# Two transformer blocks on one core: dummy matmuls and a split load ahead of the first unit, another order of steps around the two norms and in the second attention

## The chip, the cores and the metric

The kernel runs on one core of one Trainium2 chip. The metric is the device time of one execution in microseconds, from the chip's own clock; lower is better. TensorE does the matmuls and the transposes; VectorE (DVE), ScalarE (ACT) and GpSimd (POOL) do the work per element; SyncE (SP) and sometimes ACT and POOL issue the DMAs. Each engine works off its own list of instructions in the order written, and waits on semaphores where the program says so.

## The reference

Two blocks follow each other on an activation of 256 tokens x 2048 columns, all in fp32.

```python
def first_block(x, ...):
    h = rms_norm(x, pre_mix_g)
    a, gate, q, k, v = split(h @ w_in)
    yc = silu(layer_norm(depthwise_conv31(a * sigmoid(gate))))
    ya = neighbourhood_attention(q, k, v, rpb)          # 16 heads of 64
    x = x + rms_norm(concat(yc, ya) @ w_out, post_mix_g)
    h = rms_norm(x, pre_mlp_g)
    f = square(relu(h @ w_up)) @ w_down                 # 8192 wide
    return x + rms_norm(f, post_mlp_g)

def second_block(x, ...):
    h = rms_norm(x, norm_g)
    q_a, k_a, v_a, o_a, i_a, f_a, z_a, c_q, c_kv, k_r, z_b, g_a, g_b = split(h @ w_in)
    y_a = (sigmoid(o_a) * rms_norm(mlstm(...)) * silu(z_a)) @ w_a      # 8 heads
    q_b, k_b, v_b = latent_projections(c_q, c_kv, k_r)                 # norms, rotary part of 64
    y_b = (causal_attention(q_b, k_b, v_b) * silu(z_b)) @ w_b          # 16 heads
    return x + (sigmoid(g_a) * y_a + sigmoid(g_b) * y_b) @ w_out
```

## The kernel before

**Units.** All weights are cut into stripes of 512 output columns, and each stripe into units of 2 x 128 rows of the contraction: a tile of 128 x 1024 floats, 512 KB (one narrow stripe, "small", is cut otherwise). There are 734 units. Every one goes through the same four stations: SP loads it into one of 4 `raw` buffers; ACT writes its rounded high half `whi` (`split`); DVE writes the rest `wlo = raw - whi` (`low`); both have rings of 5. TensorE multiplies in `dense(u, j, tiles)`: for each of the two 128-row parts j and each of the two token tiles t, three matmuls of 128 x 512 (high x high, high x low, low x high). So a unit is 12 matmuls. The activations are held transposed in the same two halves, `ta_hi`/`ta_lo` and `tb_hi`/`tb_lo`.

**Order.** Nothing is scheduled at run time. Each engine's program walks through "slots", two for a unit; `E(name)` is the slot in which a stripe ends. All other work is written as generators ("sides") that yield the slot from which their next step may be issued; at each slot an engine first works off its sides, in the order of its list, and then the splits or lows of that slot. The order of the list decides who comes first within a slot, and an instruction that waits holds up all that is behind it on its engine.

**The beginning.** SP loads a piece of the transposed x (`xt`, 256 KB for two of its 16 rows of tiles) and unit 0, then the next piece and unit 1, and so on; ACT's queue loads `vec`, all small vectors in one table of 540 columns (270 KB). ACT then scales two tiles of xt by the gains in that table into `ta_hi` and splits unit 0; DVE makes `ta_lo` and `wlo`; then TensorE can start.

**The norms.** B1 is the first unit of the up projection, B2 that of the second block; b stands for either. The four units before b (TAIL) and the four from b on (HEAD) are multiplied tile by tile: first all four for token tile 0, then all four for tile 1. So the norm of tile 0 runs while TensorE works on tile 1, and the other way round. Steps of one norm for a tile t: DVE adds the last stripes' sums from PSUM (`finish`, L1566); ACT takes sums of squares; DVE and POOL form the root (`root`, L1443, L1444, L2105); DVE multiplies by the post gain (`gain`, L1560) and adds to x for each of four column chunks c (`add(t, c)`, L1597); TensorE transposes the chunk (L673); ACT writes `ta_hi` (L1068) and DVE `ta_lo` (`low_of(t, c)`, L1604). `NORM_TURNS` gives the slots, relative to 2b, of the eight (t, c): -2, -1, 2, 3, 5, 6, 8, 9. Two stripes end late before the first norm (mixq2, mixq3), one before the second (down73).

**The second attention.** For each of 16 heads TensorE forms scores (L797, L798), DVE masks and takes maxima (part "m", L1997 to L2002), ACT the exponentials (L1372), TensorE transposes them into PSUM bank 1 (L805), ACT copies, TensorE multiplies by v (L812 to L814), also into bank 1, and DVE scales the result out of it (part "x", L2016). Within DVE's list `uqr_side`, the rotary part of the queries of the second half (squares L1906 and L1908, then per tile t five operations L1930 to L1935), stands ahead of `at_side`.

## Time and profile before

| what | value |
|---|---|
| median of three executions | 2186.52 us (2183.7 to 2187.66) |
| the profiled execution: its time, its span | 2183.4 us, 2181.6 us |
| TensorE busy | 2157.3 us, 99% |
| DVE, ACT, POOL busy | 1345.7, 1078.5, 59.1 us |
| mean granted clock of TensorE | 1.000 |
| DMA | 419.9 MB, 192 GB/s over the span |

The span runs from the first to the last instruction in one profiled execution; the execution's own time is 1.8 us longer. Busy time of TensorE is the union of its matmuls' spans.

### The profile page before, as it was taken

The numbers are of one execution on the slowest core, as the hardware profiler recorded it, in microseconds if no ns is written. First come the engines' busy times: TensorE is split into PE (matmuls) and PEld (weight loads), VectorE is DVE, ScalarE is ACT, GpSimd is POOL, SyncE is SP. The second block draws the span as 40 slices with busy tenths as digits, with TensorE's granted clock in tenths as the row PEclk, the third lists the DMA queues.
The fourth block names the chain that finished last, engine by engine and source line by source line (L and its number), as shares of the span: only waits on it lengthen the run. The fifth ranks groups of instructions, "written<-read, shape, count | busy, mean of one in ns | idle before, by whom it ended". The sixth has DMA issues, their size and how long they took to land.

```text
span 2181.6 us, 27377 instructions
## 1 busy us (share of the span) xinstructions
PE 2157.3 (99%) x9970; PEld 1786.6 (82%) x9970; DVE 1345.7 (62%) x1795; ACT 1078.5 (49%) x1500; POOL 59.1 (3%) x70
## 2 busy tenths in 40 slices
PE   8999999999999999999999999999999999999999
PEld 6888887888888888888878888888888888788887
DVE  5898857655555555555677545556445666666764
ACT  6545565654443444444565445554444555564442
POOL 0000100000000000000000000000000000000000
PEclk9999999999999999999999999999999999999999
DMA  9565446556666565666565765556666564555975
GB/s 321 183 187 166 144 154 209 186 185 192 210 186 195 187 190 187 191 186 192 175 195 193 213 192 178 177 175 185 203 201 201 175 192 141 168 174 177 326 239 164
DMA packets 117541, 419.90 MB, mean 192 GB/s; under 512 B 13208, under 2 KB 13472, under 8 KB 117152
## 3 DMA queue, kind: packets, MB, share of 16 engines
q1 hardware_dynamic: 115520, 412.10, 59.8%
q0 software_dynamic: 1744, 5.77, 0.9%
q8 instruction: 81, 1.33, 0.3%
q14 instruction: 52, 0.43, 0.1%
q10 hardware_dynamic: 144, 0.28, 0.0%
HBM read 407.60 MB, written 10.49 MB: 192 GB/s over the span
## 4 chain that ended last, share of the span: by engine, by line
PE 81%; DVE 2%; issue 0%; ACT 0%; POOL 0%; ACTq 0%; DVEq 0%
PE g L578 25%; PE g L580 25%; PE g L579 25%; PE s L557 2%; PE s L798 0%; PE s L797 0%; DVE wlo L1429 0%; DVE ta_lo L1604 0%; PE s L805 0%; DVE arena L1597 0%; PE s L673 0%; ACT whi L897 0%; PE s L739 0%; PE s L740 0%; PE s L738 0%
## 5 line engine op out<-in xcount | busy, mean ns | idle before, releaser
L1429 DVE TENSOR_TENSOR wlo<-raw,whi 128x1024 fp32r<-128x1024 f32 x734 | 894.4, 1223 | 607.9 <-ACT whi L897 606.2
L897 ACT ACTIVATE whi<-raw 128x1024 fp32r<-128x1024 f32 x734 | 773.1, 1058 | 663.7 <-PE g L580 655.1
L578 PE MATMUL g<-whi,ta_hi 128*128 128x512 f32 x1920 | 764.6, 398 | 11.5 <-DVE wlo L1429 9.2
L580 PE MATMUL g<-whi,ta_lo 128*128 128x512 f32 x1920 | 749.7, 390 | 0.0
L579 PE MATMUL g<-wlo,ta_hi 128*128 128x512 f32 x1920 | 748.2, 390 | 0.0
L578 PEld LDWEIGHTS g<-whi,ta_hi 128*128 128x128 f32 x1920 | 361.2, 188 | 84.9 <-issue 13.2
L580 PEld LDWEIGHTS g<-whi,ta_lo 128*128 128x128 f32 x1920 | 360.7, 188 | 77.1
L579 PEld LDWEIGHTS g<-wlo,ta_hi 128*128 128x128 f32 x1920 | 361.6, 188 | 71.7
L578 PE MATMUL g<-whi,tb_hi 128*128 128x512 f32 x1008 | 399.0, 396 | 0.2 <-ACT arena L1079 0.2
L580 PE MATMUL g<-whi,tb_lo 128*128 128x512 f32 x1008 | 393.1, 390 | 0.0
L579 PE MATMUL g<-wlo,tb_hi 128*128 128x512 f32 x1008 | 392.5, 389 | 0.0
L580 PEld LDWEIGHTS g<-whi,tb_lo 128*128 128x128 f32 x1008 | 189.2, 188 | 40.2
L579 PEld LDWEIGHTS g<-wlo,tb_hi 128*128 128x128 f32 x1008 | 189.6, 188 | 37.7
L578 PEld LDWEIGHTS g<-whi,tb_hi 128*128 128x128 f32 x1008 | 189.4, 188 | 37.7 <-ACT arena L1079 0.5
L1491 DVE SCALAR_TENSOR_TENSOR arena<-arena,vc 128x256 f32<-128x256 f32 x240 | 102.4, 491 | 0.0
L2105 POOL TENSOR_TENSOR stat<-stat,ps 128x2 f32<-128x2 f32 (+3 forms) x24 | 33.1, 1381 | 1610.5 <-DVE stat L1444 727.3
L557 PEld LDWEIGHTS s<-cst,stage 128*128 128x128 f32 x384 | 47.3, 140 | 12.9 <-ACT stage L873 0.8
L557 PE MATMUL s<-cst,stage 128*128 128x128 f32 x384 | 57.5, 272 | 0.0
L873 ACT ACTIVATE stage<-g,stat 128x512 f32<-128x512 f32 x60 | 38.0, 687 | 24.7 <-PE g L580 24.7
L1566 DVE TENSOR_TENSOR arena<-arena,g 128x512 f32<-128x512 f32 x64 | 41.2, 684 | 10.0 <-PE g L580 10.0
L1432 DVE TENSOR_TENSOR tb_lo<-s,tb_hi 128x512 fp32r<-128x512 f32 x40 | 27.7, 692 | 25.3 <-ACT tb_hi L885 24.5
L885 ACT ACTIVATE tb_hi<-s 128x512 fp32r<-128x512 f32 x40 | 23.9, 598 | 37.6 <-PE s L557 37.6
(216 smaller groups left out, 914.9 us busy)
## 6 DMA issues: line engine op xcount, KB each, us to landing
raw<-in_w_in SPq DMA_DIRECT2D x320, 512.0 KB, 4.1
raw<-in_w_up SPq DMA_DIRECT2D x128, 512.0 KB, 3.6
raw<-in_w_down SPq DMA_DIRECT2D x128, 512.0 KB, 3.5
raw<-in_w_out SPq DMA_DIRECT2D x64, 512.0 KB, 4.0
raw<-in_w_a SPq DMA_DIRECT2D x32, 512.0 KB, 4.3
raw<-in_w_b SPq DMA_DIRECT2D x32, 512.0 KB, 4.5
raw<-in_w_ukv SPq DMA_DIRECT2D x16, 512.0 KB, 4.1
raw<-in_w_uq SPq DMA_DIRECT2D x12, 512.0 KB, 3.6
```

Of the source, the lines that this page charges most:

```text
L557: ins = e.transpose(b[:, k * 256 + t * P:k * 256 + (t + 1) * P], src[:, t, c:c + P], ident)
L578: e.matmul(o, xh, wh, start=first, stop=False)
L579: e.matmul(o, xh, wl, start=False, stop=False)
L580: ins = e.matmul(o, xl, wh, start=False, stop=last)
L873: ins = e.activation(dst[:, t], gps[st.pair][t][:, 0:dst.shape[2]], ACT.Copy, scale=r[:, t:t + 1])
L885: return e.activation(T[:, kt:kt + 2, :], two(b), ACT.Copy, scale=scale)
L897: e.activation(whi[u % RING][:, 0:n], raw[u % RAW][:, 0:n], ACT.Copy).then_inc(s_hi, 1)
L1429: e.tensor_tensor(l, r, h.bitcast(F32), ALU.subtract).then_inc(s_lo, 1)
L1432: return e.tensor_tensor(lo[:, kt:kt + 2, :], two(b), hi[:, kt:kt + 2, :].bitcast(F32), ALU.subtract)
L1491: e.scalar_tensor_tensor(CV[:, ct, :], UT[:, ct, j:j + 256], vec("w_dw", ct * 31 + j), CV[:, ct, :], ALU.mult, ALU.add).then_inc(cv, 1)
L1566: ins = e.tensor_tensor(f, f, gps[st.pair][t][:, :], ALU.add)
L2105: alone(e.tensor_tensor(r, v, half[:, 0:v.shape[1]], ALU.pow), rs_out, i + 1)
```

## The change

It touches five places.

- **Beginning.** The first two units and the first four tiles of xt are loaded, split and multiplied by halves (`load_half`, `split_half`, `low_half`); the semaphores count them one by one (`split_at`; x_h and x_l now count 16 steps). The first tile of xt and a table of 16 gains (8 KB) go on ACT's queue; the rest of `vec` (262 KB) is issued by SP after four units. DVE's first instruction fills `junk` with zeros; TensorE then multiplies it by itself five times (256 columns four times, 128 once, fp32), and ACT runs one activation on it.
- **Norms, DVE.** Where two stripes end late, the first is finished for tile 0 two slots earlier; `finish(1)` moves ahead of `low_of(0, 1)`; the gains of the last stripes move behind the root, those of tile 1 to just ahead of the add that reads them; `add(0, 3)` moves one slot later; the lows of units b+4 to b+8 come 4, 2, 2, 2, 2 slots later than done_slot says (before: b+4 one, the others none).
- **Norms, TensorE and ACT.** The transposes of chunk 0 of either tile come half a slot later, which in TAIL and HEAD is now a place of its own between the two parts of a unit. ACT's squares for x1 and x2 are spread over turns 3, 5 and 7 instead of 5 and 7, and those of tile 1's last stripes move from slot 2b+2 to 2b-1. Squares of mixq0 and mixq1 come one slot later.
- **Second attention.** `at_side` goes ahead of `uqr_side` in DVE's list, and the rotary steps of the second half move from slots 2 and 5 to 4 and 8 behind uqr1.
- **Table product.** `gqk` is formed just before the stripe gate0 ends, no longer first.

The diff, cut to its core:

```diff
+        def split_at(u, j=1):
+            return 2 * u + j + 1 if u < 2 else u + 3
...
+            behind = {b + m: n for b in HEAD for m, n in ((3, 1), (4, 4), (5, 2), (6, 2), (7, 2), (8, 2))}
...
-                at.setdefault(slot + late * (v - 3 in HEAD or v - 4 in HEAD), []).append(v)
+                at.setdefault(slot + late * behind.get(v, 0), []).append(v)
...
 # TensorE: norm_side, and its main program
-                    yield 2 * b + slot
+                    yield 2 * b + slot + (c == 0) / 2
...
+            q.wait_ge(dve_own, 1)
+            for n in (256, 256, 256, 256, 128):
+                e.matmul(sps[3][:, 0:n], junk[:, 0:P], junk[:, 0:n], start=True, stop=True)
...
                             for j in range(2):
                                 dense(u + i, j, (t,))
-                            for g in sides:
-                                g.upto(2 * u + 4 * t + i)
+                                for g in sides:
+                                    g.upto(2 * u + 4 * t + i - (j == 0) / 2)
...
 # ACT
+            def split_half(u, j):
+                q.wait_ge(*((d_half[u], 16) if j == 0 else (d_raw[u], 16)))
+                e.activation(whi[u][:, j * NB:(j + 1) * NB], raw[u][:, j * NB:(j + 1) * NB], ACT.Copy).then_inc(s_hi, 1)
...
+                for kt in range(16):
+                    p = kt // 2
+                    yield 2 * p - 9 + (kt % 2) * (p < 2)
+                    q.wait_ge(*((d_x0, 16) if kt == 0 else (d_xt[p], 16)))
+                    q.wait_ge(d_gain0, 16)
+                    e.activation(ta_hi[:, kt, :], XT[:, kt, :], ACT.Copy, scale=vec("pre_mix_g", kt)).then_inc(x_h, 1)
+                    if p < 2:
+                        split_half(p, kt % 2)
...
+                if len(last) == 2:
+                    yield 2 * b - 7
+                    square(0, 0)
                 yield 2 * b - 5
-                squares(0)
+                square(0, len(last) - 1)
                 for i, (t, c, slot) in enumerate(NORM_TURNS):
+                    if i == 2:
+                        yield 2 * b - 1
+                        for m in range(len(last)):
+                            square(1, m)
                     yield 2 * b + slot
...
-                    if i in (5, 7):
-                        for n in ((0, 1), (2, 3))[i // 7]:
+                    for n in {3: (0,), 5: (1,), 7: (2, 3)}.get(i, ()):
...
-            e.dma_start(VC[:, :], d["vec"]).then_inc(d_vec, 16)
+            e.dma_start(XT[:, 0, :], d["xt"][:, 0, :]).then_inc(d_x0, 16)
+            e.dma_start(vec("pre_mix_g", 0, 16), d["vec"][:, 0:16]).then_inc(d_gain0, 16)
+            q.wait_ge(dve_own, 1)
+            e.activation(junk[:, 256:257], junk[:, 0:1], ACT.Copy)
...
 # DVE: norm_side
+                if two_last:
+                    yield 2 * b - 7
+                    finish(0, 0)
                 yield 2 * b - 5
-                finish(0)
+                finish(0, end)
+                if two_last:
+                    gained_last(0, 0)
                 root(0)
+                gained_last(0, end)
                 yield 2 * b - 4
                 add(0, 0)
                 add(0, 1)
                 yield 2 * b - 3
                 low_of(0, 0)
-                yield 2 * b - 1
-                finish(1)
+                for m in range(len(last)):
+                    finish(1, m)
+                yield 2 * b - 2
                 low_of(0, 1)
                 root(1)
                 yield 2 * b
...
                 low_of(1, 1)
+                if two_last:
+                    gained_last(1, 0)
                 add(1, 2)
                 yield 2 * b + 5
                 low_of(0, 2)
-                add(0, 3)
                 yield 2 * b + 6
                 low_of(1, 2)
+                add(0, 3)
+                yield 2 * b + 7
+                gained_last(1, end)
                 add(1, 3)
...
 # DVE: uqr_side, and its main program
-                        yield E(f"uqr{hf}") + 2 + 3 * t
+                        yield E(f"uqr{hf}") + ((2, 5), (4, 8))[hf][t]
...
-            q.wait_ge(d_vec, 16)
-            own.then(e.tensor_tensor(gqk, vec("gqn"), vec("gkn"), ALU.mult))
+            own.then(e.memset(junk[:, 0:257], 0.0))
...
-                                       lat_side(), zb_side(), uqr_side(), uqn_side(), ukn_side(), at_side(), ao_side(),
+                                       lat_side(), zb_side(), at_side(), uqr_side(), uqn_side(), ukn_side(), ao_side(),
...
 # SP
+            load_half(0, 0)
+            e.dma_start(XT[:, 1, :], d["xt"][:, 1, :]).then_inc(d_xt[0], 16)
+            load_half(0, 1)
+            load_xt(1)
+            load_half(1, 0)
+            load_half(1, 1)
+            for p in range(2, 4):
                 load_xt(p)
                 load(p)
+            e.dma_start(vec("pre_mlp_g", 0, NVEC - 16), d["vec"][:, 16:NVEC]).then_inc(d_vec, 16)
```

## Rows read from the trace of the kernel before

**Rows 1.** The page of the profile: busy time of each engine.

```profile
PE 2157.3 (99%) x9970; PEld 1786.6 (82%) x9970; DVE 1345.7 (62%) x1795; ACT 1078.5 (49%) x1500; POOL 59.1 (3%) x70
```

**Rows 2.** Waits of TensorE, whole span: us in total, times, longest.

```profile
PE g L578 <- DVE wlo L1429: 9.2, 1, 9.2
PE s L673 <- DVE arena L1597: 4.3, 3, 2.1
PE s L805 <- DVE arena L2016: 2.5, 1, 2.5
PE g L578 <- DVE ta_lo L1604: 2.1, 3, 0.9
```

**Rows 3.** Timeline, 0 to 14 us: start, us, engine, line, operation, tiles, count.

```profile
5.99 0.91 ACT L905 ACTIVATE ta_hi<-arena,vc 128x256 fp32r<-128x256 f32 x2
...
6.80 1.04 ACT L897 ACTIVATE whi<-raw 128x1024 fp32r<-128x1024 f32 x1
...
6.93 0.88 DVE L1457 SCALAR_TENSOR_TENSOR ta_lo<-arena,vc,ta_hi 128x256 fp32r<-128x256 f32 x2 [2.12 <-ACT ta_hi L905]
...
7.87 1.23 DVE L1429 TENSOR_TENSOR wlo<-raw,whi 128x1024 fp32r<-128x1024 f32 x1
...
9.20 0.77 PE L578 MATMUL g<-whi,ta_hi 128*128 128x512 f32 x1 [9.20 <-DVE wlo L1429]
...
11.04 0.63 PE L579 MATMUL g<-wlo,ta_hi 128*128 128x512 f32 x1
...
11.47 0.63 PE L580 MATMUL g<-whi,ta_lo 128*128 128x512 f32 x1
...
13.38 0.40 PE L578 MATMUL g<-whi,ta_hi 128*128 128x512 f32 x1
...
16.13 0.39 PE L578 MATMUL g<-whi,ta_hi 128*128 128x512 f32 x1
```

**Rows 4.** DMA issues between 1.17 and 1.6 us: KB each, median us to landing.

```profile
raw<-in_w_in SPq DMA_DIRECT2D x1, 512.0 KB, 4.6
```

**Rows 5.** Windows: busy us (instructions) of each engine, granted clock, DMA share, GB/s.

```profile
4.00:8.00 4.00, 0.00 (x0) 0.00 (x0) 1.17 (x4) 3.29 (x5) 0.00 (x0) 1.00 1.03 395
```

**Rows 6.** The page's DMA issues: count, KB each, median us from issue to landing.

```profile
raw<-in_w_up SPq DMA_DIRECT2D x128, 512.0 KB, 3.6
```

**Rows 7.** Timeline around the first norm.

```profile
364.67 1.42 DVE L1597 SCALAR_TENSOR_TENSOR arena<-arena,stat 128x512 f32<-128x512 f32 x2
...
369.30 1.28 DVE L1566 TENSOR_TENSOR arena<-arena,g 128x512 f32<-128x512 f32 x2
...
370.50 1.12 DVE L1604 SCALAR_TENSOR_TENSOR ta_lo<-s,vc,ta_hi 128x128 fp32r<-128x128 f32 x4
...
374.99 0.66 PE L673 MATMUL s<-cst,arena 128*128 128x128 f32 x4 [2.12 <-DVE arena L1597]
...
384.94 0.47 PE L578 MATMUL g<-whi,ta_hi 128*128 128x512 f32 x1 [0.88 <-DVE ta_lo L1604]
```

**Rows 8.** Window of the first norm; columns as in the windows above.

```profile
364.70:384.90 20.20, 16.09 (x78) 12.30 (x78) 20.07 (x42) 13.25 (x36) 0.93 (x1) 1.00 0.41 130
```

**Rows 9.** Timeline around the second norm.

```profile
1085.68 0.60 PE L673 MATMUL s<-cst,arena 128*128 128x128 f32 x4
...
1093.70 0.66 PE L673 MATMUL s<-cst,arena 128*128 128x128 f32 x4 [1.42 <-DVE arena L1597]
```

**Rows 10.** Timeline in the second attention.

```profile
1851.91 0.69 DVE L1930 TENSOR_TENSOR stage<-stage,vc 128x512 f32<-128x512 f32 x1
...
1854.76 0.55 DVE L1997 TENSOR_TENSOR arena<-s,cst 128x384 f32<-128x384 f32 x1
...
1860.14 0.55 PE L805 MATMUL s<-cst,arena 128*128 128x128 f32 x3 [2.49 <-DVE arena L2016]
...
1860.77 0.39 PE L579 MATMUL g<-wlo,ta_hi 128*128 128x512 f32 x1
...
1860.99 0.40 PE L580 MATMUL g<-whi,ta_lo 128*128 128x512 f32 x1
```

More of the change, by code:

```diff
@@ L332, in two_blocks @@
         d_xt = [sem(f"d_xt{i}") for i in range(8)]
+        d_gain0, d_x0 = sem("d_gain0"), sem("d_x0")
+        d_half = [sem(f"d_half{i}") for i in range(2)]
         d_cst, d_vec, d_pos, d_xr, d_pg, d_pg2, d_x2s, d_rows, d_f2 = (sem(n) for n in (
@@ L1421, in two, with low_half @@
                 return sps[b][:, :].rearrange("p (k n) -> p k n", k=2)
+            def low_half(u, j):
+                r, h, l = (b[u][:, j * NB:(j + 1) * NB] for b in (raw, whi, wlo))
+                q.wait_ge(s_hi, split_at(u, j))
+                e.tensor_tensor(l, r, h.bitcast(F32), ALU.subtract).then_inc(s_lo, 1)
             def low(u):
@@ L1569, in norm_side, with finish, gained_last @@
             def norm_side(b, base, last, added, squared, halves, names, ss_of, gname, ss, gained):
[L1571 to L1583 removed]
+                def finish(t, m):
+                    n, k = last[m], len(last) * t + m
+                    if t == 0:
+                        q.wait_ge(half_mm, halves + m + 1)
+                    else:
+                        q.wait_ge(s_mm, by[names[0] + str(n)].last + 1)
+                    if names[0] == "mixq":
+                        q.wait_ge(mx_b, n + 1)
+                    else:
+                        q.wait_ge(dn_a, 24 + n)
+                    add_psum(by[names[0] + str(n)], n, (t,)).then_inc(added[0], 1)
+                def gained_last(t, m):
+                    q.wait_ge(added[0], added[1] + len(last) * t + m + 1)
+                    gained[0] = gain(last[m], (t,))
                 def root(t):
@@ L1587, in root @@
                     mean_of_tile(ss_of, t, names[1] + str(t))
-                    q.wait_ge(added[0], added[1] + len(last) * (t + 1))
-                    for n in last:
-                        gained[0] = gain(n, (t,))
                 def add(t, c):
@@ L2160, in load, with load_half @@
                 e.dma_start(raw[u % RAW][:, 0:n], src).then_inc(d_raw[u % RAW], 16)
+            def load_half(u, j):
+                e.dma_start(raw[u][:, j * NB:(j + 1) * NB], d["w_in"][unit_of[u].n, u, :, j * NB:(j + 1) * NB]).then_inc(
+                    d_raw[u] if j else d_half[u], 16)
             def load_xt(p):
```

105 lines of the change are left out of this document (43 added, 62 removed).

## The prediction

> **What bounds the kernel now.** I read the page first, for who is busy: TensorE, 99% of the span [rows 1]; so only its idle time and its slow stretches can be won, some 24 us in all (span less busy time). Next the waits of TensorE, for who causes them [rows 2]: 9.2 us once for the first `wlo`; 4.3 us in three waits for an `add` of a norm and 2.1 us in three for a `ta_lo`; 2.5 us once for a DVE step of the second attention. These are the places of the change. Then the timelines at each place, for what stands in DVE's queue ahead of the awaited step, and the windows, for whether DVE or the DMA engines are full there.
>
> **Beginning.** Unit 0's load is issued at 1.18 us and lands 4.6 us later, at 5.8 [rows 4]. Behind it come ACT's two `ta_hi` (0.45 us each) and the whole split (1.04), DVE's two `ta_lo` (0.44 each) and `wlo` (1.23), and TensorE begins at 9.20 [rows 3]. By 5.8 us 256 KB of xt, 270 KB of vec and 512 KB of the unit have landed, 1038 KB; the engines move 395 GB/s then [rows 5], about 390 KB/us, so the flow counts as if begun at 5.8 - 1038/390 = 3.1 us. After the change the first part needs 128 (xt) + 8 (gains) + 256 (half a unit) = 392 KB: landed at 3.1 + 1.0 = 4.1 us. Then half a split (0.52), half a low (0.62) and some 0.2 us of handing over: TensorE begins at 5.5, 3.7 us earlier. The bounds of this unseen chain: 5.0 (the half lands at 3.6, as nothing else is waited for) and 6.4 (the gains, 128 small pieces, or sharing of the engines cost 0.9).
>
> The first matmuls start 0.43 us apart (11.04 and 11.47), 512 columns at the 1.2 GHz level; later ones 0.22 (1860.77 and 1860.99 in [rows 10]), the 2.4 GHz level. The granted clock reads 1.00 in both, so it is the intervals that tell. Unit 0 takes 13.38 - 9.20 = 4.18 us, unit 1 2.75 [rows 3]: 1.43 us lost. TensorE had then been at work for some 2.9 us. The dummies are 1152 fp32 columns; three fp32 transposes of 128 columns (L805) take 0.55 us at the full clock [rows 10], 1.4 ns a column, so 2.9 at half of it: 3.3 us together, and half of that if the clock rises at once. They wait only for a fill of 257 columns, and can run from about 1.2 us, so they end between 3 and 5 us, before anything real is ready: they delay nothing. I take the whole 1.43 us; the bound is 0, if they are too short or the clock falls again in the gap before 5.5 us. Against the fall speaks that after 2.49 us of idleness the matmuls are 0.22 apart at once [rows 10]. The Trainium skill (TensorE: Matmul & The Clock Gate, Part 1) says that the same kernel shows 6, 11 or 14 slow matmuls in different executions; by it the loss before would be 1.2 to 2.9 us, and so would the gain; no row here shows more than one execution.
>
> What is late next: the data. Units 0 to 3 and all of xt's first eight tiles with vec's first part are 3080 KB, unit 3 lands at 3.1 + 7.9 = 11.0, unit 2 at 9.0. Unit 2's split and low take 1.04 + 1.23 + 0.1, ready at 11.4 to 11.6; TensorE, at 2.72 us a unit (12 x 0.227), wants it at 5.5 + 5.45 = 10.95. I charge 0.55 (bounds 0 and 1.5). From unit 4 on, data come every 2.0 us (768 KB at 390) and are used every 2.72; so the lead grows and is kept. The DMAs issued earlier in SP's queue (halves, vec's rest) are six issues more, 0.45 us each by the spacing of its loads, hidden as the engines, not the queue, are the limit. ACT's table load lies before its first data in the new order. Sum: 3.7 + 1.43 - 0.55 = **4.6 us** gained, bounds 2.0 and 5.6.
>
> The Trainium skill (DMA: Bandwidth & Descriptors, Rules for kernel authors) says that under 64 KB a transfer pays mostly overhead. That speaks against a separate 8 KB of gains: by it they would land no sooner than a bigger piece, which the bound of 6.4 us takes in.
>
> **Second attention.** At 1851.91 DVE starts the rotary operations of tile 0; only behind them, at 1854.76, can the mask and maxima of head 7 start, though its scores were ready; TensorE, wanting head 7's transposes at 1857.65, starts them at 1860.14 after 2.49 us [rows 10], released by the "x" of head 6, which is queued behind all that. With `at_side` first and the rotary block two slots later, the mask starts about 2.8 us earlier (the whole block leaves its front), exponentials and "x" follow. The rotary blocks then lie behind "x" of heads 6 and 7; their reader, TensorE's qr transposes, stands at slot 12 behind uqr1, four slots (5.4 us) after the last block, which takes 3. Nothing else is late: **2.5 us** gained, bounds 1.5 and 2.6.
>
> **First norm.** DVE is full: 20.07 of 20.20 us [rows 8], from `add(0, 0)` at 364.67 to the `ta_lo` that TensorE awaits at 384.94 [rows 7]. TensorE loses 0.81 (what [rows 2] have for adds, less 2.12 and the second norm's 1.42) + 2.12 + 0.88 and two small waits of 0.38 and 0.12, 4.3 us in all; so what matters is what leaves DVE's queue ahead of that last need. An `add` is 0.71 (1.42 for two), a half `finish` 0.64 and a gain the same (same operation and shape), a low 1.14 behind another. Ahead of it no longer stand `add(0, 3)`, the low of b+5 and the gain of chunk 3: 0.7 + 1.15 + 0.65 = 2.5; and the whole begins 0.9 earlier, since the first stripe of tile 0 is finished and squared while the second is being multiplied. Against this, 0.9 us more waiting for `ta_hi`: ACT's squares of turn 3 now stand ahead of chunk 2's. So unit b+4 begins some 2.5 us earlier in relation to the work before it. Then 0.8 is given back: `low_of(1, 3)` now stands behind a gain, two adds and the low of b+7, and TensorE waits for it at unit b+6 (0.85, was 0.12). `finish(1)` ahead of `low_of(0, 1)` makes a wait of 0.6 at the third HEAD unit, another of 0.5 for the low of b+3, and takes the 2.12 at `add(1, 0)` down to 0.2. Walking the four queues step by step at these durations I get waits of 2.5 instead of 4.3: **1.8 us** gained, bounds -0.5 and 3.3.
>
> **Second norm.** One late stripe, so no earlier finish; chunk 0's transposes were in time at 1085.68 [rows 9] and now come 0.68 us (three matmuls) later, which delays their `ta_lo` to about 0.25 after its need. The 1.42 us at `add(1, 0)` [rows 9] shrinks to 0.1 and a wait of 0.4 for a low arises; the 0.89 at b+4 becomes 0.7; at b+5 and b+6 come new waits of 0.35 and 0.8 as above. Sum 2.6 against 2.3 by this walk, within its error; half of what the first norm gives would be 0.9. I take **0.2 us** gained, bounds -1.0 and 1.2.
>
> **Sum.** 4.6 + 2.5 + 1.8 + 0.2 = 9.1 us. The profiled execution took 2183.4 us, which gives 2174.3; it lies 3.1 under the median of the three runs, and the median less 9.1 is 2177.4. I predict **2177 us**. A measurement can tell about 0.2%, 4.4 us, from no change.
>
> **Rivals.** (a) The forecast, gain 7 to 11.5: chance 0.63. (b) The beginning is bound by data and keeps the slow clock: start at 6.4, no clock gain, 1.0 for unit 2, so 2.8 - 1.0 = 1.8 instead of 4.6; total 6.3, 2180 us. For it: the engines at 395 GB/s; against: less than half of the bytes are needed at first. 0.14. (c) The norms turn one full queue into another: each loses 1 us instead of winning, total 7.1 - 2 = 5, 2181.5. For it: DVE is full, and moving work creates none; against: the lows taken out have time. 0.09. (d) The change doesn't come through, (b) and (c) together or less: gain 0 to 4, 2184. 0.10. (e) Slower: a low that comes up to four slots later frees its `raw` buffer later, the load of b+8 is issued about 3 us later, and a load takes 3.6 us to land [rows 6]. By my walk it lands a good 1 us before its split and ACT and DVE have 4 us more before TensorE wants it; so it decides only from landings of 8.6 us on, and would have to cost 7 us at each of two norms to outweigh the rest: 2191 or more. 0.04.
>
> **How the numbers follow.** (a) and (b) span 2174.5 to 2180.5; with (c), and 1.5 us for what executions differ in, the range is 2172.5 to 2182, which leaves out 0.2. Faster by over 0.2% are (a), (b) and most of (c), 0.86; within it the rest of (c) and (d), 0.10; slower 0.04.
>
> **What would show it.** First real matmul at 5.5 us and 0.23 apart at once; a first wait for unit 2; no wait ahead of head 7's transposes; waits in norm 1 summing to about 2.5 and in norm 2 to about 2.4, the last of each at unit b+6. I am wrong if the first real matmuls are 0.43 apart, if the gains land last, or if the waits behind HEAD grow beyond 2 us.

## The result, and the profile after

| | before | after |
|---|---|---|
| median (range) of 5 executions each, same chip | 2186.33 us (2183.7 to 2187.66) | 2176.29 us (2175.92 to 2176.65) |
| profiled execution: its own time / span | 2183.4 / 2181.6 us | 2175.92 / 2174.1 us |
| ratio of the times, 95% interval | | 0.9957 [0.9943, 0.9972] |

The median fell by 10.0 us, the profiled executions differ by 7.5 us. The 2.5 us between these two numbers are a finding of their own (below, under the waits filled with matmuls). First the 7.5.

The page: busy time of each engine (compare [rows 1]). TensorE is again 99% busy; its sum grew by 4.2 us, though the dummies (4.21) are no useful work.

```profile
PE 2161.5 (99%) x9980; PEld 1787.8 (82%) x9980; DVE 1346.8 (62%) x1798; ACT 1078.9 (50%) x1503; POOL 61.2 (3%) x70
```

Waits of TensorE, whole span (compare [rows 2]). L585 to L587 are the lines 578 to 580 of before, L680 is 673, L812 is 805, L1632 is 1604, L1447 the low of half a unit; L845 are the dummies.

```profile
PE s L662 <- DVE arena L1520: 2.0, 1, 2.0
PE g L585 <- DVE ta_lo L1632: 1.4, 3, 0.5
PE g L585 <- issue: 1.3, 3, 0.8
PE s L845 <- DVE junk L2107: 1.2, 1, 1.2
PE g L585 <- DVE wlo L1447: 1.2, 1, 1.2
PE s L680 <- DVE arena L1625: 0.8, 4, 0.2
```

The 9.2 us for the first `wlo` are now 1.2 and 1.2 around 4.2 us of dummies; the 4.3 for the `add` of a norm are 0.8, the 2.1 for a `ta_lo` are 1.4, and the 2.5 of the second attention are gone. The longest single wait is now the first line, in the layer norm. The change leaves it as it was; [rows 2] do not have it. In the kernel before (TensorE's timeline):

```profile
262.19 1.09 PE L655 MATMUL s<-cst,arena 128*128 128x128 f32 x8 [1.99 <-DVE arena L1491]
```

To see where the time went I subtracted, for each of the 8832 matmuls of the weight units (8784 of them on the lines 585 to 587), its start after from its start before. Where this shift changes, time was won or lost:

| stretch | shift behind it | change | predicted |
|---|---|---|---|
| first matmul (9.20 to 6.56) | 2.64 | +2.64 | +3.7 |
| end of unit 0's and 1's slow stretch | 3.98 | +1.34 | +1.43 |
| unit 2 waits for its data | 2.94 | -1.04 | -0.55 |
| first norm | 5.16 | +2.2 | +1.8 |
| second norm | 5.21 | +0.05 | +0.2 |
| head 7's transposes | 8.09 (5.53 ahead of it) | +2.56 | +2.5 |
| four units further | 7.57 | -0.52 | 0 |

(Between the second norm and the attention it drifts by 0.3.)

**Beginning.** Timeline, 0 to 14 us: start, us, engine, line, operation, tiles, count (compare [rows 3]).

```profile
1.19 4.21 PE L845 MATMUL s<-junk 128*128 128x256 f32 x10 [1.19 <-DVE junk L2107]
...
1.66 1.28 ACT L1419 ACT_TABLE_LOAD   x1 [1.66 <-PEq L2427]
...
4.71 0.51 ACT L919 ACTIVATE ta_hi<-arena,vc 128x256 fp32r<-128x256 f32 x1 [1.55 <-DMA vc<-in_vec]
5.12 0.61 ACT L911 ACTIVATE whi<-raw 128x512 fp32r<-128x512 f32 x1
...
5.76 0.69 DVE L1447 TENSOR_TENSOR wlo<-raw,whi 128x512 fp32r<-128x512 f32 x1
...
6.56 0.47 PE L585 MATMUL g<-whi,ta_hi 128*128 128x512 f32 x1 [1.16 <-DVE wlo L1447]
...
6.87 0.39 PE L586 MATMUL g<-wlo,ta_hi 128*128 128x512 f32 x1
...
10.68 1.06 ACT L907 ACTIVATE whi<-raw 128x1024 fp32r<-128x1024 f32 x1 [0.43 <-DMA raw<-in_w_in]
...
13.10 0.47 PE L585 MATMUL g<-whi,ta_hi 128*128 128x512 f32 x1 [0.84 <-issue]
```

Windows: length, busy us of each engine, granted clock, DMA share, GB/s; the stretch of [rows 5] again.

```profile
4.00:8.00 4.00, 2.84 (x11) 2.16 (x10) 2.57 (x5) 2.85 (x6) 0.00 (x0) 1.00 0.96 302
```

ACT's first work waits for the gains, the last piece to land (4.62 us, behind half a unit at 4.03 and xt's first tile at 4.21). The chain is then 4.71 `ta_hi`, 5.12 `whi`, 5.76 `wlo`, 6.56 matmul. From there the matmuls start 0.23 apart (only the second comes 0.31 behind the first, as it does behind the norms' waits): the higher level at once. Unit 2 lands at 10.66, and TensorE waits for it. The DMA engines are as busy as before (0.96 against 1.03) but move 302 GB/s where they moved 395.

**First norm**, TensorE's waits in its timeline (compare [rows 7]).

```profile
367.47 0.47 PE L585 MATMUL g<-whi,ta_hi 128*128 128x512 f32 x1 [0.36 <-DVE ta_lo L1632]
...
369.32 0.47 PE L585 MATMUL g<-whi,ta_hi 128*128 128x512 f32 x1 [0.23 <-issue]
...
370.48 0.66 PE L680 MATMUL s<-cst,arena 128*128 128x128 f32 x4 [0.21 <-DVE arena L1625]
...
382.62 0.66 PE L680 MATMUL s<-cst,arena 128*128 128x128 f32 x4 [0.17 <-DVE arena L1625]
...
385.65 0.39 PE L587 MATMUL g<-whi,ta_lo 128*128 128x512 f32 x1
386.53 0.47 PE L585 MATMUL g<-whi,ta_hi 128*128 128x512 f32 x1 [0.50 <-DVE ta_lo L1632]
386.84 0.40 PE L586 MATMUL g<-wlo,ta_hi 128*128 128x512 f32 x1
```

The 2.12 and 0.88 of before are gone; small waits of 0.36, 0.23 and 0.21 stand at the third HEAD unit, the low of b+3 and `add(1, 0)`, and the last, 0.50, at unit b+6, each at a place where the prediction had one; the 0.17 it had not. The last three lines show that a wait costs more than is listed: the starts are 0.88 and 0.31 apart instead of 0.23 each, so the 0.50 costs 0.73.

**Second attention** (compare [rows 10]): head 7's transposes, without a wait, while the rotary block begins beside them; and the place where 0.5 us is given back.

```profile
1851.91 0.68 DVE L1970 TENSOR_TENSOR stage<-stage,vc 128x512 f32<-128x512 f32 x1
1852.05 0.55 PE L812 MATMUL s<-cst,arena 128*128 128x128 f32 x3
...
1860.40 1.22 DVE L1455 TENSOR_TENSOR wlo<-raw,whi 128x1024 fp32r<-128x1024 f32 x1
...
1861.54 0.68 DVE L1458 TENSOR_TENSOR tb_lo<-s,tb_hi 128x512 fp32r<-128x512 f32 x1
...
1862.32 0.63 PE L564 MATMUL s<-cst,stage 128*128 128x128 f32 x4 [0.31 <-issue]
```

The reader of the rotary result has it (the block's last addition ends at 1860.48). It starts at 1862.32, 0.1 us after the end of a `tb_lo` that reads the PSUM banks of the turns; before, that `tb_lo` ended at 1868.67, 1.3 us ahead of the same reader at 1869.93. It now stands behind the delayed rotary block and a `wlo`.

### The profile page after: what moved, and what is told of

Read it like the earlier page. It is cut to its first block, busy times and chain, and to the rows that moved or that the text cites. A ratio compares the mean times of both kernels' runs of the same rounds, so it can differ in the third digit from the quotient of the medians.

```text
span 2174.1 us, 27413 instructions
## 1 busy us (share of the span) xinstructions
PE 2161.5 (99%) x9980; PEld 1787.8 (82%) x9980; DVE 1346.8 (62%) x1798; ACT 1078.9 (50%) x1503; POOL 61.2 (3%) x70
## 3 DMA queue, kind: packets, MB, share of 16 engines
q8 instruction: 81, 1.33, 0.2%
## 4 chain that ended last, share of the span: by engine, by line
PE 96%; DVE 2%; ACT 1%; issue 1%; DMA 0%; POOL 0%; ACTq 0%; DVEq 0%
PE g L585 30%; PE g L587 30%; PE g L586 30%; PE s L564 2%; PE s L642 1%; DVE wlo L1455 0%; PE s L805 0%; PE s L804 0%; DVE arena L1520 0%; DVE ta_lo L1632 0%; PE s L624 0%; PE s L634 0%; PE s L812 0%; PE s L680 0%; ACT whi L907 0%
## 5 line engine op out<-in xcount | busy, mean ns | idle before, releaser
L585 PE MATMUL g<-whi,ta_hi 128*128 128x512 f32 x1920 | 764.0, 398 | 4.3 <-DVE ta_lo L1632 1.4
L587 PE MATMUL g<-whi,ta_lo 128*128 128x512 f32 x1920 | 749.0, 390 | 0.0
L585 PEld LDWEIGHTS g<-whi,ta_hi 128*128 128x128 f32 x1920 | 360.6, 188 | 79.6 <-issue 7.1
L587 PEld LDWEIGHTS g<-whi,ta_lo 128*128 128x128 f32 x1920 | 360.3, 188 | 77.3
L585 PE MATMUL g<-whi,tb_hi 128*128 128x512 f32 x1008 | 398.8, 396 | 0.2 <-ACT arena L1096 0.2
L587 PE MATMUL g<-whi,tb_lo 128*128 128x512 f32 x1008 | 393.0, 390 | 0.0
L587 PEld LDWEIGHTS g<-whi,tb_lo 128*128 128x128 f32 x1008 | 189.2, 188 | 40.3
L585 PEld LDWEIGHTS g<-whi,tb_hi 128*128 128x128 f32 x1008 | 189.3, 188 | 37.8 <-ACT arena L1096 0.5
```

The lines of the kernel that those rows point to most:

```text
L585: e.matmul(o, xh, wh, start=first, stop=False)
L587: ins = e.matmul(o, xl, wh, start=False, stop=last)
```

## The experiments

The theory: four parts add up, each at its own place, as in the table. Rivals: the dummies do nothing; the norms' gain comes from elsewhere; the extra 2.5 us of the medians come from a part that the profile doesn't show. The kernel before was measured again beside the experiments: its median was 2186.64 us beside the first four, 2186.80 beside the next four, and 2187.02 beside the last four. With every execution its mean granted clock is recorded. In the profiles it reads 0.999 where the clock fell once behind a wait; a slow beginning does not lower it.

### Without the dummies

```diff
-            q.wait_ge(dve_own, 1)
-            for n in (256, 256, 256, 256, 128):
-                e.matmul(sps[3][:, 0:n], junk[:, 0:P], junk[:, 0:n], start=True, stop=True)
```

> The changed kernel without the five dummy matmuls. Theory: the first real matmul still starts at 6.6 us (data set it), but 0.43 us apart until TensorE has been at work for some 3 us, so unit 2's matmuls find their data ready and the 0.84 us wait there takes part of the loss: profile 0.5 to 1.4 us longer, about 1 us. Rival 1: the dummies do nothing (the clock would rise or fall by itself): no change. Rival 2: the dummies are also what made the executions agree (spread 0.7 us, against 4.0 before): then the single times scatter over 2 us or more again and the median is 2 to 4 us longer.

Measured: 2178.34 us (2176.61 to 2179.42), ratio 0.996 [0.9947, 0.9972]. Timeline of TensorE:

```profile
6.76 0.76 PE L585 MATMUL g<-whi,ta_hi 128*128 128x512 f32 x1 [6.76 <-DVE wlo L1444]
7.32 0.63 PE L586 MATMUL g<-wlo,ta_hi 128*128 128x512 f32 x1
7.75 0.63 PE L587 MATMUL g<-whi,ta_lo 128*128 128x512 f32 x1
```

The matmuls are 0.43 apart up to 10.3 us, and there is no wait for unit 2. At units 2 and 3 the kernel is only 1.0 and 0.9 us behind the changed one: of the clock's 1.34 us a part is taken back by the wait for data. A further 1.4 us is lost at 260 us, in the layer norm, where nothing was edited: the granted clock reads 0.50 there from 259.8 to 263.2 us, eight transposes take 1.97 us instead of 1.09 (0.8 of the 1.4), and the matmuls behind them are 0.43 apart. Together this is the 2.4 us between the two profiled executions. This was the first hint of the scatter.

The times alone do not show what the dummies are worth: the two ratios' intervals overlap, and the two executions at a mean clock of 1.0 (2176.61 and 2176.67) lie only 0.3 us above the changed kernel's at that clock (2176.33, median of the eight in its two measurements). The median's 2.05 us come mostly from three executions with a fall, more than the 1.4 expected.

### The dummies alone, in the kernel before

```diff
-        GQK = 1
+        GQK = 2
...
+            q.wait_ge(dve_own, 1)
+            for n in (256, 256, 256, 256, 128):
+                e.matmul(sps[3][:, 0:n], junk[:, 0:P], junk[:, 0:n], start=True, stop=True)
...
+            own.then(e.memset(junk[:, 0:257], 0.0))
```

> The kernel before with nothing but the fill and the five dummy matmuls, which end at about 5.4 us while the first real matmul stays at 9.2. Theory: the clock stays up through the 3.8 us gap, matmuls 0.23 apart from the first, 1.43 us gained in the profile. Rival 1: the clock falls back in the longer gap, and nothing is gained. Rival 2, on scatter: if the slow first matmuls are what spreads the times of the kernel before over 4 us, the single times agree within 1 us here and the median falls by 3 us or more.

Measured: 2187.2 us (2183.64 to 2187.69), ratio 1.0 [0.9991, 1.0009]. Timeline:

```profile
1.19 4.21 PE L838 MATMUL s<-junk 128*128 128x256 f32 x10 [1.19 <-DVE junk L2070]
9.25 0.77 PE L578 MATMUL g<-whi,ta_hi 128*128 128x512 f32 x1 [3.85 <-DVE wlo L1432]
```

The granted clock rose at 5.8 us, fell again at 9.2 behind 3.85 us of idleness, and the first real matmuls are slow as before: the theory failed and rival 1 came out. Without the early start the dummies are worth nothing; the early start works without them (the run above: 6.76 instead of 9.20).

### The second attention's order of before

```diff
-                        yield E(f"uqr{hf}") + ((2, 5), (4, 8))[hf][t]
+                        yield E(f"uqr{hf}") + ((2, 5), (2, 5))[hf][t]
...
-                                       lat_side(), zb_side(), at_side(), uqr_side(), uqn_side(), ukn_side(), ao_side(),
+                                       lat_side(), zb_side(), uqr_side(), uqn_side(), ukn_side(), at_side(), ao_side(),
```

> The changed kernel with the order of before in the second attention (side list and rotary slots). Theory: the 2.5 us wait ahead of head 7's transposes is back, and the 0.5 us that was given back behind it goes: 2.1 to 2.6 us longer in profile and median. Rival: the wait was hidden by other slack that the earlier stages now leave, and under 1 us comes back.

Measured: 2180.57 us (2179.87 to 2182.04), ratio 0.9974 [0.9963, 0.9984]: 4.3 above the changed kernel's median, more than the 2.5 expected. Timeline of TensorE and windows:

```profile
1855.66 0.55 PE L812 MATMUL s<-cst,arena 128*128 128x128 f32 x3 [2.50 <-DVE arena L2056]
...
1856.51 0.55 PE L587 MATMUL g<-whi,ta_lo 128*128 128x512 f32 x1
1856.85 0.63 PE L585 MATMUL g<-whi,ta_hi 128*128 128x512 f32 x1
...
1860.15 0.39 PE L587 MATMUL g<-whi,ta_lo 128*128 128x512 f32 x1
```

```profile
1856.00:1858.00 2.00, 2.00 (x8) 1.63 (x7) 1.97 (x4) 1.44 (x2) 0.00 (x0) 0.65 0.88 246
1858.00:1860.00 2.00, 2.00 (x6) 1.54 (x6) 1.93 (x4) 0.00 (x0) 0.00 (x0) 0.50 0.77 203
```

The wait of 2.50 us is back, and the 0.5 us given back behind it is gone. New is that the clock is taken away behind the wait: nine starts from 1856.51 on are 0.34 to 0.43 apart and not 0.23, which costs 1.6 us. In the profile of before the same wait left the clock at its upper level [rows 10]. So a wait of this length costs its own 2.5 us in one execution and 4.1 in another. The median's 4.3 above the changed kernel is mostly that: none of the seven executions here has a mean clock of 1.0, where eight of the changed kernel's ten have. The profile is 4.6 longer, as it also has a slow beginning (0.6) and 0.5 of small shifts up to the attention.

### The norms' order of before

```diff
-            behind = {b + m: n for b in HEAD for m, n in ((3, 1), (4, 4), (5, 2), (6, 2), (7, 2), (8, 2))}
+            behind = {b + m: n for b in HEAD for m, n in ((3, 1), (4, 1))}
...
-                    yield 2 * b + slot + (c == 0) / 2
+                    yield 2 * b + slot
```

and the steps of ACT's and DVE's `norm_side` in the order of before.

> The changed kernel with the steps, slots and lows of before at both norms. Theory: the waits of before are back, 4.3 us at the first norm against 2.1 and no change at the second: 2.2 us longer, all of it between units 110 and 118. Rival: as TensorE reaches the norm 2.9 us earlier, DVE is later in relation to it and more comes back than was won, 3 us or more, or some at the second norm too.

Measured: 2178.84 us (2178.36 to 2180.29), ratio 0.9965 [0.9953, 0.9978]. TensorE's timeline at the first norm:

```profile
362.88 0.66 PE L680 MATMUL s<-cst,arena 128*128 128x128 f32 x4 [0.81 <-DVE arena L1623]
...
368.65 0.47 PE L585 MATMUL g<-whi,ta_hi 128*128 128x512 f32 x1 [0.37 <-DVE ta_lo L1630]
...
372.39 0.66 PE L680 MATMUL s<-cst,arena 128*128 128x128 f32 x4 [2.11 <-DVE arena L1623]
...
382.35 0.47 PE L585 MATMUL g<-whi,ta_hi 128*128 128x512 f32 x1 [0.90 <-DVE ta_lo L1630]
```

The waits of before are back one by one. By the shifts the first norm loses 2.3 us and the second 0.15, as expected: the sizes of the table, from the other side. The run takes all steps of the norms back at once, so it doesn't say what each of them gave.

### Waits filled with matmuls in the kernel before

If a long wait lets the clock fall in some executions only, then the kernel before should scatter, and matmuls in the waits should stop that, though they are more work. Six, six and eight unused 128-column matmuls, behind the layer norm's, the first norm's and head 7's last work:

```diff
+                    for _ in range(6 if g == 0 else 0):
+                        e.matmul(b[:, 0:P], ident, ident, start=True, stop=True)
...
+                    if i == 2 and base == X1:
+                        s = bank(0)
+                        for _ in range(6):
+                            e.matmul(s[:, 0:P], ident, ident, start=True, stop=True)
...
+                        if i == 7:
+                            b = bank(2)
+                            for _ in range(8):
+                                e.matmul(b[:, 0:P], ident, ident, start=True, stop=True)
```

> The kernel before, all its waits kept, with idle matmuls of the identity put into its three waits of 2 us and more: 6 ahead of the first LayerNorm transposes, 6 ahead of the chunk 0, tile 1 transposes of the first norm, 8 ahead of head 7's transposes; about 0.22 us each. Theory, formed from the last runs: in most executions the clock falls in one of these waits and the matmuls behind it are 0.43 us apart for a while, 0.7 to 1.7 us each time; that is the 2.8 us by which the median of before lies above its profiled execution. With TensorE busy in the waits this cannot happen: the profile stays at 2183.4 to 2184, all single times lie within 1 us and the median falls to 2183.5 to 2184.5, though work was added. Rival: the scatter has another source (DMA, memory): single times still spread from 2183.7 to 2187.7, the median stays at 2186.6 or rises by what was added.

Measured: 2184.27 us (2183.72 to 2186.25), ratio 0.9993 [0.9984, 1.0002]. Waits of TensorE:

```profile
PE s L679 <- DVE arena L1607: 3.0, 3, 1.4
...
PE s L815 <- DVE arena L2026: 0.7, 1, 0.7
PE s L657 <- DVE arena L1501: 0.6, 1, 0.6
```

The ratio's interval just touches 1, but the median is 2.5 us below that of before beside it (2186.80). What settles it is the mean granted clock. The 41 executions of the kernel before for which it is on record fall into three groups without overlap:

| mean granted clock | before | with its waits filled |
|---|---|---|
| 1.0 | 9: 2183.43 to 2183.99 | 11: 2183.72 to 2186.25 |
| 0.999 | 13: 2186.13 to 2186.80 | none |
| 0.998 | 19: 2187.02 to 2188.27 | none |

Filling took the falls from 32 of 41 executions to none of 11. That the highest filled times still reach 2186.25 is another matter: the spans of all eleven are 2181.6 to 2182.9 us long, and two of the times lie 3.4 and 3.6 us above their span instead of about 2; the cause of that is open.

The profiled execution of before, 2183.4, is at 1.0 too, so its trace shows none of the falls that most executions have. The changed kernel was at 1.0 in all five executions of its first measurement. Compared at equal clock, the two kernels' medians are 2183.81 (nine executions) and 2176.33 (eight, with those of its second measurement, the control below): 7.5 us, what the traces add up to. The other 2.5 us of the medians go with the falls; two of the three waits (2.12 and 2.49 us) the change removed. How the 2.5 are made up is not shown, as no profile of before caught a fall. In the profiles that did, a fall costs 1.4 us in the layer norm and 1.6 in the second attention, and none is seen behind the first norm's wait; but the medians of the other two groups (2186.45 and 2187.46) lie 2.6 and 3.7 us above that of the first. So about 1 us of the first step is more than a fall was seen to cost. It may be the beginning: the three profiles of kernels with early start and dummies that have a fall (the attention's order of before, and two below, unit 1 whole and the later low) all have a slow beginning too.

### The gains loaded first; unit 1 loaded whole

The gains land last: does that set the start? And do two loads of half a unit delay unit 2?

```diff
-            e.dma_start(XT[:, 0, :], d["xt"][:, 0, :]).then_inc(d_x0, 16)
             e.dma_start(vec("pre_mix_g", 0, 16), d["vec"][:, 0:16]).then_inc(d_gain0, 16)
+            e.dma_start(XT[:, 0, :], d["xt"][:, 0, :]).then_inc(d_x0, 16)
```

> The changed kernel with the 8 KB of gains issued ahead of the first tile of xt on ACT's queue. Theory: the gains landed last, at 4.62 us, behind xt at 4.21 and the half unit at 4.03, because their issue came 0.45 us later; now the tile of xt is last and the first real matmul starts 0.0 to 0.3 us earlier (6.3 to 6.5); behind the wait for unit 2 nothing of it is left, as that is set by data: the total changes by under 0.2 us. Rival: each small piece costs the engines as much wherever it stands, and nothing moves even at the first matmul.

Measured: 2177.43 us (2175.99, 2176.71, 2178.15, 2178.41), ratio 0.996 [0.9945, 0.9975]. The gains land at 4.16 us, but xt's tile now at 4.70, and the first matmul starts at 6.57 as before: whichever is second in the queue lands last. No difference.

```diff
-            load_half(1, 0)
-            load_half(1, 1)
+            load(1)
```

> The changed kernel with unit 1 loaded in one transfer of 512 KB (rows of 4 KB) in place of two halves (rows of 2 KB); its splits and lows stay halved. Theory: the engines moved 288 to 336 GB/s between 4 and 9 us against 395 to 406 before, because of the shorter rows; with one transfer unit 2 lands at about 10.2 in place of 10.66 and the wait of 0.84 at unit 2 shrinks by 0.3 to 0.5. Rival: unit 1 itself is then late, as its first half waits for the whole, and a new wait of some 0.3 us at unit 1 takes the place: no change.

Measured: 2177.22 us (2176.54, 2176.72, 2177.73, 2178.41), ratio 0.9958 [0.9945, 0.9972]. Unit 1 is there at 8.97 us in place of 7.47 and 8.17, unit 2 at 10.90 and not earlier (10.66 with the halves). The expected gain did not come. But the trace has a hole, 98 GB/s from 5 to 6 us against 291 in the changed kernel's (packets of up to 1.4 us, begun at 4.5), and from 6 to 8 us it moves 354 and 361 GB/s where the changed kernel moves 336 and 293. So it neither shows nor refutes that the halves of unit 1 hold up unit 2. Its profile also has a slow beginning, which hides what the later unit 1 would cost, and the layer norm's fall.

### The low of HEAD unit b+7 one slot later

The remaining wait at unit b+6 was predicted to come from DVE doing the low of b+7 ahead of `low_of(1, 3)`.

```diff
-            behind = {b + m: n for b in HEAD for m, n in ((3, 1), (4, 4), (5, 2), (6, 2), (7, 2), (8, 2))}
+            behind = {b + m: n for b in HEAD for m, n in ((3, 1), (4, 4), (5, 2), (6, 2), (7, 3), (8, 2))}
```

> The changed kernel with the low of unit b+7 one slot later, so that low_of(1, 3) goes ahead of it at both norms. Theory: the last wait of each norm, 0.50 and 0.52 us at unit b+6, stands behind that low of 1.22 us and goes: 0.8 to 1.0 us less in all. Rival: ACT's ta_hi of (1, 3) is itself late, so DVE idles and the wait stays at 0.3 or more.

Measured: 2174.99 us (2174.74, 2174.86, 2175.11, 2176.7), ratio 0.9949 [0.9936, 0.9963]. The waits at b+6 are gone at both norms, and each gives 0.73 us by the shifts, 1.5 in all: more than the two waits of 0.5 and than the 0.8 to 1.0 expected, since from start to start each wait cost 0.73 and 0.76 (above, at the first norm). Its profiled execution, 2176.7, has the fall behind the layer norm (its wait of 1.97 us; TensorE's timeline and windows):

```profile
260.15 1.97 PE L662 MATMUL s<-cst,arena 128*128 128x128 f32 x8 [1.97 <-DVE arena L1520]
261.77 0.78 PE L585 MATMUL g<-whi,tb_hi 128*128 128x512 f32 x1
262.34 0.63 PE L586 MATMUL g<-wlo,tb_hi 128*128 128x512 f32 x1
```

```profile
260.00:262.00 2.00, 1.85 (x9) 1.85 (x10) 1.29 (x3) 0.60 (x1) 0.00 (x0) 0.50 0.03 8
```

### The changed kernel again, more dummies, the layer norm's wait filled

Three questions on what is left of the scatter: was the changed kernel's 0.7 us luck; do dummies that reach up to the first real matmul settle the beginning; and is the layer norm's wait of 2.0 us the place of the falls? The first is the changed kernel as it is.

> The changed kernel once more, for its scatter. Its first five executions lay within 0.73 us (2175.92 to 2176.65), while three kernels that differ from it by one small edit scattered over 2 us or more (the one with the gains loaded first from 2175.99 to 2178.41). If the granted clock falls behind long waits in some executions of it too, this one scatters alike: median 2176.3 to 2177.5 us, highest above 2177.5. If its own timing avoids the falls, all executions lie within 0.8 us of 2176.2.

Measured: 2176.63 us (2175.99 to 2178.52), ratio 0.9959 [0.9946, 0.9971]; two of five executions at 0.999 (2178.06 and 2178.52). The narrow first measurement was luck; the median moved by 0.3 us. In its profile the first matmuls are slow up to 10.2 us, behind the same dummies. Its two executions with a fall lie 1.7 and 2.2 us above 2176.33.

```diff
-            for n in (256, 256, 256, 256, 128):
+            for n in (256, 256, 256, 256, 256, 128):
```

> 1408 columns of dummies in place of 1152: at 3.65 ns a column (4.21 us for 1152) they end at about 6.3 us, close to the first real matmul at 6.56 and not 1.2 us before it. If the clock at the beginning depends on the gap behind the dummies, the first real matmuls are 0.22 us apart in the profile, and no execution carries the 0.6 us of a slow beginning: median 2175.9 to 2176.3, scatter no larger than that of the kernel it is compared with. Rival: the level at the beginning depends on something else in the execution, and the median and the scatter stay as they are. Other side: the dummies end later than reckoned and push the first matmul back, at most 0.3 us, median up to 2176.8.

Measured: 2177.31 us (2175.51 to 2178.56), ratio 0.9959 [0.9946, 0.9971]; three of five at 0.999. Timeline:

```profile
1.19 5.06 PE L845 MATMUL s<-junk 128*128 128x256 f32 x12 [1.19 <-DVE junk L2107]
6.78 0.47 PE L585 MATMUL g<-whi,ta_hi 128*128 128x512 f32 x1 [0.53 <-DVE wlo L1447]
7.09 0.40 PE L586 MATMUL g<-wlo,ta_hi 128*128 128x512 f32 x1
```

The profile has its first matmuls at the upper level, but neither median nor scatter is better: the expectation failed. A full start does not settle the 2 to 3 us between executions.

```diff
+                    for _ in range(6 if g == 0 else 0):
+                        e.matmul(b[:, 0:P], ident, ident, start=True, stop=True)
                     q.wait_ge(cv, 240)
```

> Six 128-column matmuls of the identity are put where TensorE waits 2.0 us for the layer norm's step of VectorE; their result is not used. If the 0.7 us that three profiles show behind that wait (matmuls 0.43 us apart from 259.8 to 263.2 us) is a fall of the clock that comes of idleness, it is gone in every execution: median 0.2 to 0.7 us below the changed kernel's of the same call, lowest time as before (2175.9). Rival: the clock falls there whatever TensorE does, or was no part of the scatter: no difference in the median. Other side: six matmuls cost up to 0.3 us themselves if the wait is not longer than they are.

Measured: 2176.62 us (2176.05 to 2178.07), ratio 0.9955 [0.9942, 0.9969]. The median is that of the control (2176.63): no gain shown, and a miss of what was expected. (The fall costs 1.4 us, as said above; the 0.7 left out the transposes.) But all five are at 1.0. The 2178.07 is the profiled execution: its wait is 0.6 us, the clock holds behind it, and 2.1 us are lost at the beginning, with matmuls 0.43 apart up to 13 us.

### The best of these together

The later low, the longer dummies and the filled wait, the three edits above in one kernel.

> The changed kernel with the low half of HEAD unit b+7 one slot later, the longer dummies and the matmuls in the layer norm's wait. Parts: 0.73 us at each of two norms (1.46), shown in the profile of the kernel that had this edit alone, and no slow stretch at the beginning and behind the layer norm. If they add up: profile and lowest at 2174.4, median 2174.3 to 2174.9, thus 1.5 to 2.5 below the changed kernel and 11 to 12 below the kernel before. If the fillers do nothing, the median is that of the later low alone, 2175.0, scattering up to 2176.7.

Measured: 2174.55 us (2174.37 to 2175.16), ratio 0.9947 [0.9935, 0.996]: 2.1 below the control, 12.5 below before, and the narrowest of the last four; the profiled execution is the highest of the five, 2175.16 and not the 2174.4 expected. All five at 1.0. Its first matmul starts at 6.58, at the upper level. TensorE's timeline:

```profile
13.80 0.47 PE L585 MATMUL g<-whi,ta_hi 128*128 128x512 f32 x1 [1.49 <-issue]
...
259.99 1.09 PE L664 MATMUL s<-cst,arena 128*128 128x128 f32 x8 [0.60 <-DVE arena L1522]
```

Its lowest time is 1.55 below the changed kernel's lowest (2175.92), the 1.46 of the two lows. Unit 2's wait is 1.49 here, because its load landed at 11.36 us (10.66 in the profile of the changed kernel, 10.92 in the control's, 11.27 with more dummies): the landing itself differs by 0.7 us between executions.

Taking all kernels with the changed kernel's steps and the layer norm's wait unfilled (the changed one, its control, the gains first, unit 1 whole, the later low, more dummies), 17 of 27 executions are at 1.0; with the wait filled, 10 of 10. If filling did nothing, all ten falls in 37 executions would miss the ten filled ones in about one of forty such samples. So the filling probably holds the clock here, as it did in the kernel before. What it is worth in the mean, 0.5 us by an estimate (10 of 27 times the 1.4 us of a fall), five executions do not show.

## Why the prediction held, and where its steps did not

The forecast was 2177 us, a range of 2172.5 to 2182, and a gain; measured are 2176.29 and, in the control, 2176.63. Rival (a), the forecast, came out. But two errors of opposite sign lie under it: the steps promised 9.1 us and gave 7.5, and the executions of before had on top about 2.5 us that no step speaks of. That the sum is off by less than 1 us is in part luck.

**The start** was mis-sized: 6.56 us, not 5.5. The prediction named its own sign of failure ("if the gains land last"), and it applies: they landed at 4.62, not 4.1 (+0.52). The chain behind them left out ACT's half `ta_hi`, which stands ahead of the split (0.41 from 4.71 to 5.12), and half a split and half a low took 0.61 and 0.69 instead of 0.52 and 0.62 (+0.16). The order of the two transfers is no matter, as the run with the gains first shows. The separate 8 KB took 3.4 us from issue to landing, beside 3.3 and 3.5 for 256 and 128 KB. That agrees with what the Trainium skill (DMA: Bandwidth & Descriptors, Rules for kernel authors) says, that under 64 KB a transfer pays mostly overhead. The upper bound of 6.4 was 0.2 too low.

One cause at the start was passed over. Before, ACT had its table to load when its first data came:

```profile
4.69 1.28 ACT L905 ACT_TABLE_LOAD   x1 [4.69 <-DMA vc<-in_vec]
```

So its two `ta_hi` began at 5.99, and the split behind them only at 6.80, though unit 0 was there at 5.80. The prediction counted the `ta_hi` as work behind the unit's landing. With the one activation on `junk` the table is loaded from 1.66 on. By these rows that alone would have let the split begin at 5.80, 1.0 us earlier (an estimate; no run has the activation without the halves). So a part of the 2.64 us is not due to the halves.

**Unit 2** lands at 10.66, not 9.0. The step that failed is "about 390 KB/us": the engines move 302 GB/s from 4 to 8 us where they moved 395 [rows 5]. The shorter rows are not the reason by their own price: in the packet records of both traces a typical packet of 2 KB takes 84 ns and one of 4 KB 159 ns, so two halves cost 6% more than a whole. The loss lies mostly in single long packets: from 4 to 9 us 77 of 607 packets of 2 KB took over 100 ns and fill 19.3 of the 63.9 us of packet time; before it was 13 of 257, with 3.0 of 23.5 us. Why they are long is open; in both traces they are rare from 9 us on, and the rate is then 397 GB/s and more. The loss is 1.04, inside its bounds of 0 and 1.5. Rival (b), a beginning bound by data, was half right: the start is that late, but the clock's gain came through in the profiled execution.

**The clock at the beginning**: +1.34 of 1.43 in the profile. But of eight profiles with these same dummies and the early start only three have their first real matmuls 0.23 apart, five have them 0.43 apart up to 10 or 13 us. So the 1.34 is the best case. At unit 3 those eight are between 0 and 2.05 us behind the changed kernel's profile, 0.7 in the mean; the profile without dummies is 0.9 behind. What the dummies give in a mean execution is thus hardly shown, neither by the traces nor by the times. The prediction's argument that the clock survives a gap of 2.49 us [rows 10] rested on one execution; with that wait put back into the changed kernel all seven executions have a fall. The Trainium skill's rule (TensorE: Matmul & The Clock Gate, Part 1), that the count of slow matmuls differs between executions of one kernel, fits here: none in the changed kernel's profile, about eight in the control's. What limits the loss is that unit 2 lands so late: the control's slow beginning puts unit 2 only 0.76 us behind, of which 0.61 are seen with a fast beginning too (more dummies), when the load lands late.

**The attention** was right: 2.56 against 2.5. "Nothing else is late" was wrong: a `tb_lo` behind the moved rotary block frees the banks for the next turns 0.5 us late. That this is the cause is read from the order of times in one trace and from its absence with the old order, and was not tried alone.

**The norms** came out as walked: 2.2 against 1.8, and 0.05 against 0.2, confirmed from the other side as 2.3 and 0.1. In the first, waits of 4.3 became 1.7, not 2.5: the two at the third HEAD unit and at b+6 were taken at 0.6 and 0.85 and are 0.36 and 0.50. The walk's cause for the last one, the low of b+7 ahead of `low_of(1, 3)`, is shown by the run that moves it. In the second norm the waits shrank by 1.0 (2.31 to 1.33) and the time by next to nothing. From start to start the two waits of before cost 2.8 us and the six of after 2.7: each costs some 0.2 us more than is listed, whatever its length (at unit b+6 0.73 for a listed 0.50), and there are four more of them. In the first norm the same count gives 5.5 and 3.3, the 2.2 of the table, where the listed waits fell by 2.6. The walk added up waits as they are listed, and would miss that elsewhere too. What the single steps of the norms gave was not tried, the low of b+7 excepted.

**The scatter** is what the prediction did not have. It noticed that the profiled execution lay 3.1 us under the median and carried that difference over unchanged to the new kernel. In fact it goes with the falls of the clock behind long waits, and the change removed two of these waits; about 1 us of it no trace explains. That the difference carried over came near the mark (2.5 of 3.1) for a reason that the prediction did not know.

## What to carry to other kernels

A wait of TensorE of about 2 us or more had two prices here, its own length and, in a part of the executions, 1.4 to 1.6 us for the half clock behind it; before pricing such a wait from one trace, look whether the profiled execution lies at the bottom of the measured times. Where the wait can't be removed, a few unused matmuls in it are cheap insurance. Several short waits can cost as much as one long one: compare starts, not listed waits. When a full queue is reordered, list for every step that moves back what is queued behind it and what buffer that frees, and look at who waits last in the new order: here one entry of a table, one slot later, gave 1.5 us, which is more than all the other steps gave in the second norm (0.05).

## What the runs showed of the hardware that was not expected

- The granted clock was 0.50 behind the layer norm's wait of only 1.97 us in one profile (matmuls 0.43 apart from 262.34 on) and stayed at 1.00 behind the same wait of 1.99 us in others, with the same instructions; it also stayed at 1.00 behind 2.49 us [rows 10].
- More work gave less time: 20 unused matmuls in the kernel before lowered its median from 2186.80 to 2184.27 us, though its lowest time rose from 2183.43 to 2183.72; the shortest span is 2181.6 us with and without them.
- At about the same busy share (0.96 and 1.03) the DMA engines moved 302 GB/s with half units in the mix and 395 with the loads of before. A packet of 2 KB typically takes 84 ns and one of 4 KB 159 ns, so row length explains 6%; single packets of 0.1 to 0.7 us make up most of the rest.
- 1152 columns of fp32 dummies took 4.21 us, 3.65 ns a column, not the 2.9 ns reckoned as twice the price at the full clock; they ended at 5.40, still ahead of all real work.
